# Seven half-wide products for two output blocks in six iterations of the last up projection

## The chip, the cores and the metric

The kernel runs on one core of a Trainium2 chip. The metric is the device time of one execution in microseconds (us), the median over runs; lower is better.

## What is computed

Three transformer blocks on 512 tokens of width 1024, all in float32, chained: a short convolution mixer, an attention block, and a block with gated linear attention beside window attention, each followed by a feed-forward part. The change lies in the last feed-forward part:

```python
h2 = _rms_norm(x, norm_ffn_g[l])
gu = h2 @ w_ffn_in[l]
ff_gate, ff_up = gu[..., :D_FF_2], gu[..., D_FF_2:]
x = x + (jax.nn.silu(ff_gate) * ff_up) @ w_ffn_out[l]
```

with h2 512 x 1024 and w_ffn_in 1024 x 5632 (D_FF_2 = 2816, which is 22 blocks of 128 columns on each side). The left half of the columns goes through silu (the "a" side, or silu side), the right half is the factor (the "g" side).

## The kernel before

Activations lie transposed: features on the 128 partitions, the 512 tokens along the free axis. Every float32 operand of a product is split into a high part (rounded to TensorE's fp32r form) and a low part (the rest), and each product is three matmuls: high weight by high activation, high weight by low activation, low weight by high activation. A *unit* of weights is one block of 128 output features by up to 1024 inputs (8 k tiles of 128 x 128, 512 KB). It takes this path:

- SyncE (SP) loads it into a landing buffer RAW (two of them in these phases, used in turn), as soon as GpSimd has split the unit that lay there.
- GpSimd (POOL) splits it into one slot of a ring of four (WH high, WL low): per half of the unit a TENSOR_SCALAR (L555, high) and a TENSOR_TENSOR (L558, low), four operations in all. It first waits until TensorE is through with the unit that lies in the slot. `WeightPhase` (L69) holds these counts; `owner` remembers the last unit of a slot over the borders of phases.
- TensorE (`unit`, L567 to L578) waits for the split, runs 8 x 3 matmuls of 128x512 into one PSUM bank and counts the unit as done.

The last up projection is phase `up2`: 11 iterations of four units (a, g, a, g), with banks 0 to 3, for two of the 22 blocks m. Its `body` (L639 on TensorE) waits before each unit until VectorE has emptied the bank. VectorE (DVE, `ffn`, L1794) multiplies the a result by the tokens' norm factor W[0] (L1804), then g (L1810), multiplies g by the silu of a (L1813) and makes the low part HL of that (L1815); ScalarE (ACT, L1321) makes the silu (L1328) and the high part HH (L1331). HH and HL, 44 KB a partition each, are filled block by block and feed the down projection. Every engine runs its own program in order; semaphores alone tie them together.

```python
pe.matmul(o, WH[s][:, k, :], xh[:, k0 + k, :], start=first and k == 0, stop=False)
pe.matmul(o, WH[s][:, k, :], xl[:, k0 + k, :], start=False, stop=False)
mm = pe.matmul(o, WL[s][:, k, :], xh[:, k0 + k, :], start=False, stop=last and k == nk - 1)
```

## Time and profile before

| | |
|---|---|
| median of 3 runs | 2083.39 us (2083.32 to 2083.63) |
| span of the profiled execution | 2081.4 us, so 2.0 us of the time lie outside the span |
| TensorE busy | 2074.3 us, 100% of the span |
| GpSimd busy | 1515.7 us, 73% |
| VectorE busy | 969.0 us, 47% |
| ScalarE busy | 499.3 us, 24% |

The span runs from the first to the last instruction of the profiled execution, whose own time stands nowhere else; the median of the runs stands for it. Busy is the union of an engine's instructions. A matmul's record is longer than the time until the next one may start, since matmuls are pipelined: what a matmul costs is read from the distance of two starts.

### The profile page before, as it was taken

The numbers are of one execution on the slowest core, as the hardware profiler recorded it, in microseconds if no ns is written. First come the engines' busy times: TensorE is split into PE (matmuls) and PEld (weight loads), VectorE is DVE, ScalarE is ACT, GpSimd is POOL, SyncE is SP. The second block draws the span as 40 slices with busy tenths as digits, with TensorE's granted clock in tenths as the row PEclk, the third lists the DMA queues.
The fourth block names the chain that finished last, engine by engine and source line by source line (L and its number), as shares of the span: only waits on it lengthen the run. The fifth ranks groups of instructions, "written<-read, shape, count | busy, mean of one in ns | idle before, by whom it ended". The sixth has DMA issues, their size and how long they took to land.

```text
span 2081.4 us, 28663 instructions
## 1 busy us (share of the span) xinstructions
PE 2074.3 (100%) x10112; PEld 1731.8 (83%) x10112; DVE 969.0 (47%) x1459; ACT 499.3 (24%) x999; POOL 1515.7 (73%) x1607
## 2 busy tenths in 40 slices
PE   9999999999999999999999999999999999999999
PEld 8888888888788878888888888889888888888887
DVE  6566655521456675655542166436753243222100
ACT  2002111100267673211100054222353122111000
POOL 7888888867865547888877775546545788777675
PEclk9999999999999999999999999999999999999999
DMA  5333333323333223333323332223222333333233
GB/s 158 101 89 102 95 101 91 101 84 93 106 108 86 82 82 86 91 101 91 100 86 94 100 90 81 62 71 102 72 68 69 87 110 93 99 93 101 86 91 96
DMA packets 368163, 192.45 MB, mean 92 GB/s; under 512 B 8672, under 2 KB 364608, under 8 KB 368080
## 3 DMA queue, kind: packets, MB, share of 16 engines
q1 hardware_dynamic: 365280, 186.52, 31.2%
q10 hardware_dynamic: 2800, 4.83, 0.7%
q8 instruction: 52, 0.85, 0.2%
q14 instruction: 31, 0.25, 0.0%
HBM read 189.19 MB, written 2.13 MB: 92 GB/s over the span
## 4 chain that ended last, share of the span: by engine, by line
PE 97%; DVE 2%; ACT 1%; DMA 0%; issue 0%; SPq 0%; DVEq 0%; ACTq 0%
PE PS L575 22%; PE PS L577 22%; PE PS L576 22%; PE PS L892 3%; PE PS L894 3%; PE PS L893 3%; PE PS L908 2%; PE PS L909 2%; PE PS L910 2%; PE PS L734 1%; PE PS L735 1%; PE PS L736 1%; PE PS L697 1%; PE PS L1091 1%; PE PS L677 1%; PE PS L762 1%
## 5 line engine op out<-in xcount | busy, mean ns | idle before, releaser
L558 POOL TENSOR_TENSOR RING<-RAW,RING 128x512 fp32r<-128x512 f32 x704 | 976.1, 1386 | 58.7
L555 POOL TENSOR_SCALAR RING<-RAW 128x512 fp32r<-128x512 f32 x704 | 519.6, 738 | 342.9 <-PE PS L894 89.9
L575 PE MATMUL PS<-XH,RING 128*128 128x512 f32 x1296 | 504.8, 389 | 0.0
L576 PE MATMUL PS<-XL,RING 128*128 128x512 f32 x1296 | 504.2, 389 | 0.0
L577 PE MATMUL PS<-XH,RING 128*128 128x512 f32 x1296 | 504.2, 389 | 0.0
L575 PEld LDWEIGHTS PS<-XH,RING 128*128 128x128 f32 x1296 | 243.3, 188 | 51.3 <-issue 1.1
L576 PEld LDWEIGHTS PS<-XL,RING 128*128 128x128 f32 x1296 | 243.3, 188 | 50.6 <-issue 0.2
L577 PEld LDWEIGHTS PS<-XH,RING 128*128 128x128 f32 x1296 | 243.3, 188 | 50.5
L575 PE MATMUL PS<-HH,RING 128*128 128x512 f32 x528 | 205.6, 389 | 0.0
L577 PE MATMUL PS<-HH,RING 128*128 128x512 f32 x528 | 205.4, 389 | 0.0
L576 PE MATMUL PS<-HL,RING 128*128 128x512 f32 x528 | 205.4, 389 | 0.0
L1785 DVE TENSOR_TENSOR XT<-PS,XT 128x512 f32<-128x512 f32 (+1 forms) x47 | 32.5, 692 | 325.7 <-PE PS L577 325.7
L553 POOL TENSOR_TENSOR COL<-COL 128x1 f32<-128x1 f32 x195 | 41.3, 212 | 147.1 <-PE PS L577 136.7
L1328 ACT ACTIVATE W<-W 128x512 f32<-128x512 f32 x66 | 41.7, 632 | 393.6 <-DVE W L1792 309.4
L577 PEld LDWEIGHTS PS<-HH,RING 128*128 128x128 f32 x528 | 99.1, 188 | 20.6
L575 PEld LDWEIGHTS PS<-HH,RING 128*128 128x128 f32 x528 | 99.1, 188 | 20.5
L576 PEld LDWEIGHTS PS<-HL,RING 128*128 128x128 f32 x528 | 99.1, 188 | 20.5
L1810 DVE TENSOR_TENSOR W<-PS,W 128x512 f32<-128x512 f32 x66 | 45.5, 690 | 147.0 <-PE PS L577 147.0
L1804 DVE TENSOR_TENSOR W<-PS,W 128x512 f32<-128x512 f32 x66 | 45.6, 691 | 129.8 <-PE PS L577 129.7
L1314 ACT ACTIVATE W<-XT 128x512 f32<-128x512 f32 (+1 forms) x40 | 25.3, 634 | 317.7 <-DVE XT L1785 242.1
L892 PE MATMUL PS<-XH,RING 128*128 128x512 f32 x232 | 95.2, 410 | 0.0
L908 PE MATMUL PS<-RING,XH 128*128 128x256 f32 x320 | 92.2, 288 | 0.0
(342 smaller groups left out, 3405.3 us busy)
## 6 DMA issues: line engine op xcount, KB each, us to landing
RAW<-in_ffn_w_up SPq DMA_DIRECT2D x88, 512.0 KB, 3.7
RAW<-in_w_in SPq DMA_DIRECT2D x52, 512.0 KB, 3.7
RAW<-in_w_ffn_in SPq DMA_DIRECT2D x44, 512.0 KB, 3.7
RAW<-in_ffn_w_down SPq DMA_DIRECT2D x32, 512.0 KB, 3.8
RAW<-in_a_w_in SPq DMA_DIRECT2D x24, 512.0 KB, 3.6
RAW<-in_b_w_qg SPq DMA_DIRECT2D x16, 512.0 KB, 3.6
RAW<-in_w_kvf SPq DMA_DIRECT2D x16, 512.0 KB, 3.9
RAW<-in_w_ffn_out SPq DMA_DIRECT2D x16, 512.0 KB, 3.7
```

The costliest lines, as they stand in the source:

```text
L555: hi = pool.tensor_scalar(WH[s][:, k0_:k1, :], RAW[r][:, k0_:k1, :], 1.0, 1.0, ALU.mult, ALU.mult)
L558: lo = pool.tensor_tensor(WL[s][:, k0_:k1, :], RAW[r][:, k0_:k1, :], WH[s][:, k0_:k1, :].bitcast(F32), ALU.subtract)
L575: pe.matmul(o, WH[s][:, k, :], xh[:, k0 + k, :], start=first and k == 0, stop=False)
L576: pe.matmul(o, WH[s][:, k, :], xl[:, k0 + k, :], start=False, stop=False)
L577: mm = pe.matmul(o, WL[s][:, k, :], xh[:, k0 + k, :], start=False, stop=last and k == nk - 1)
L892: pe.matmul(o, WH[s][:, k, :], xh[:, k, :], start=k == 0, stop=False)
L893: pe.matmul(o, WH[s][:, k, :], xl[:, k, :], start=False, stop=False)
L894: mm = pe.matmul(o, WL[s][:, k, :], xh[:, k, :], start=False, stop=k == KT - 1)
L908: pe.matmul(o, XH[:, k, c], RING[:, s:s + 2, 0, k, :], start=k == 0, stop=False)
L1328: act.activation(u, u, ACT.Silu).then_inc(sem("ffn_silu"), 1)
L1804: dve.tensor_tensor(a[:, 2:S + 2] if with_conv else u, PS[:, 2 * q, :], W[0][:, 0:S], ALU.mult).then_inc(sem("ffn_a"), 1)
L1810: dve.tensor_tensor(g, PS[:, 2 * q + 1, :], W[0][:, 0:S], ALU.mult).then_inc(sem("ffn_g"), 1)
```

## The change

Iterations 2 to 7 of `up2` (6 of 11) get a phase of their own, `seven2`, between two iterations of the old form and three of the old form (`rest2`).

In `seven2` the two a blocks (256 output features by 1024 inputs by 512 tokens) are made as a 2 x 2 by 2 x 2 product by Winograd's form of Strassen's scheme: seven products of quarters (128 outputs by 512 inputs by 256 tokens) in place of eight. Each is 4 k tiles x 3 matmuls of 128x256. The two g blocks keep their 128x512 matmuls, counted in halves of four k tiles. So an iteration has eleven *uses* of half a ring slot (`SEVEN_USES`), 7 + 4, and the ring is run as eight halves; uses 0 to 6 are the products. A use is freed by TensorE alone.

- Weights: both a units and both g units land in four RAW buffers. VectorE makes three sums of quarters (`add_weights`), GpSimd the fourth (right behind the low part of use 4, in place over a quarter of RAW0). ScalarE writes the high parts of all uses (`round_use`), GpSimd their low parts (`seven_low`).
- Activations: four combinations of quarters of the normed input, once for all six iterations, in HH's and HL's space that is still free: ScalarE one scaled quarter (four operations of 128x256) and the four high parts (128x1024), VectorE 16 operations of 128x256 and four low parts of 128x1024, between `body(0)` and `body(1)`.
- Results: ScalarE copies bank 0 after use 0 (`P1`) and after use 4; VectorE adds the products up (five operations of 128x256), multiplies the two sums by W[0] from SBUF, and goes on as before. Uses 4 and 6 add onto banks 0 and 3. TensorE waits before use 4 for the copy P1 (`taken`), before use 6 for VectorE's third sum.

Also the other semaphores are shared anew under fewer names; RAW has a fourth buffer; all six iterations are written out in every engine's program. The core of the diff:

```diff
+SEVEN = range(2, 8)
+SEVEN_USES = 11
+HALF = 256
...
+        TH = at("TH", [P, 4, 4, HALF], F32R, BIG + 28 * KB)
+        TL = at("TL", [P, 4, 4, HALF], F32R, BIG + 72 * KB)
+        TF = [at(f"TF{c}", [P, 4, HALF], F32, BIG + (8 + 4 * c) * KB) for c in range(5)]
+        SUM1, SUM2 = [at(f"SUM{k}", [P, 4, P], F32, W_at[8 + k]) for k in range(2)]
+        P1, U2, U3 = W[7][:, 0:HALF], W[7][:, HALF:S], W[1][:, 0:HALF]
...
+        def seven_phases(l):
+
+            ua, ug = [(up[l], 0, KT, col(q * P, 2 * P)) for q in range(2)], [(up[l], 0, KT, col(FF + q * P, 2 * P)) for q in range(2)]
+            plain = [ua[0], ug[0], ua[1], ug[1]]
+            a = wphase(4, SEVEN.start, plain)
+            b = wphase(4, len(SEVEN), ua + ug, landing=4, start=SEVEN.start)
+            stream["skip"] += b.U * b.iters
+            last = SEVEN_USES * len(SEVEN)
+            for slot in range(4):
+                of = []
+                for n in range(last - 8, last):
+                    if n % 8 // 2 == slot:
+                        t, q = divmod(n, SEVEN_USES)
+                        of.append(b.unit(SEVEN.start + t, 1 if q < 7 else 2 + (q - 7) // 2))
+                stream["owner"][slot] = max(of)
+            c = wphase(4, FT // 2 - SEVEN.stop, plain, start=SEVEN.stop)
+            return a, b, c
...
+        def ring_half(n):
+
+            h = n % 8
+            return h // 2, slice(h % 2 * 4, h % 2 * 4 + 4)
+
...
+        SEVEN_SRC = [RAW[0][:, 0:4, :], SUM2[:, :, :], RAW[1][:, 0:4, :], SUM1[:, :, :], RAW[0][:, 4:8, :], RAW[1][:, 4:8, :],
+                     RAW[0][:, 4:8, :], RAW[2][:, 0:4, :], RAW[2][:, 4:8, :], RAW[3][:, 0:4, :], RAW[3][:, 4:8, :]]
...
+            def seven_low(p):
+
+                for t in range(len(SEVEN)):
+                    for q in range(SEVEN_USES):
+                        n = SEVEN_USES * t + q
+                        s, k = ring_half(n)
+                        pool.wait_ge(sem("high_made"), KT + n + 1)
+                        lo = pool.tensor_tensor(WL[s][:, k, :], SEVEN_SRC[q], WH[s][:, k, :].bitcast(F32), ALU.subtract)
+                        lo.then_inc(use_count(p, n, sem("low_made"), split_done, 9, KT)[0], 2 if q == 6 else 1)
+                        if q == 4:
+                            pool.wait_ge(sem("low_made"), use_count(p, n, sem("low_made"), split_done, 9, KT)[1])
+                            pool.tensor_tensor(RAW[0][:, 4:8, :], SUM2[:, :, :], RAW[0][:, 4:8, :], ALU.subtract).then_inc(
+                                sem("low_made"), 1)
...
+            def seven_products(l):
+
+                p = ph["seven2"]
+                xs = [(XH[:, 0:4, 0:HALF], XL[:, 0:4, 0:HALF]), (TH[:, 1], TL[:, 1]), (TH[:, 2], TL[:, 2]), (TH[:, 0], TL[:, 0]),
+                      (XH[:, 4:8, 0:HALF], XL[:, 4:8, 0:HALF]), (TH[:, 3], TL[:, 3]), (XH[:, 4:8, HALF:S], XL[:, 4:8, HALF:S])]
+                bank = (0, 1, 2, 3, 0, 4, 3)
+                for t, i in enumerate(SEVEN):
+                    m = l * FT + 2 * i
+                    for q in range(7):
+                        n = SEVEN_USES * t + q
+                        s, ks = ring_half(n)
+                        pe.wait_ge(*use_count(p, n, sem("low_made"), split_done, 9, KT))
+                        if q == 4:
+                            pe.wait_ge(sem("taken"), TB + 2 * t + 1)
+                        elif q == 6:
+                            pe.wait_ge(sem("combined"), KT + 5 * t + 3)
+                        elif t == 0:
+                            if q < 4:
+                                pe.wait_ge(sem(("ffn_a", "ffn_g")[q % 2]), m - 1 + q // 2)
+                            if q == 1:
+                                pe.wait_ge(sem("xld"), scaled(4) + KT + 4)
+                        elif q == 0:
+                            pe.wait_ge(sem("taken"), TB + 2 * t)
+                        else:
+                            pe.wait_ge(sem("combined"), KT + 5 * t - 5 + {1: 1, 2: 2, 3: 5, 5: 4}[q])
+                        xh, xl = xs[q]
+                        o = PS[:, bank[q], 0:HALF]
+                        for k in range(4):
+                            w = ks.start + k
+                            on = q in (4, 6)
+                            pe.matmul(o, WH[s][:, w, :], xh[:, k, :], start=not on and k == 0, stop=False, skip_group_check=on)
+                            pe.matmul(o, WH[s][:, w, :], xl[:, k, :], start=False, stop=False, skip_group_check=on)
+                            mm = pe.matmul(o, WL[s][:, w, :], xh[:, k, :], start=False, stop=k == 3, skip_group_check=on)
+                        mm.then_inc(use_count(p, n, sem("used"), unit_done, 8, 2 * KT)[0], 2 if q == 6 else 1)
+                    for u in range(2):
+                        if t > 0:
+                            pe.wait_ge(sem("ffn_g"), m - 1 + u)
+                        for h in range(2):
+                            n = SEVEN_USES * t + 7 + 2 * u + h
+                            s, ks = ring_half(n)
+                            pe.wait_ge(*use_count(p, n, sem("low_made"), split_done, 9, KT))
+                            o = PS[:, 5 + u, :]
+                            for k in range(4):
+                                w, x = ks.start + k, 4 * h + k
+                                pe.matmul(o, WH[s][:, w, :], XH[:, x, :], start=h == 0 and k == 0, stop=False)
+                                pe.matmul(o, WH[s][:, w, :], XL[:, x, :], start=False, stop=False)
+                                mm = pe.matmul(o, WL[s][:, w, :], XH[:, x, :], start=False, stop=h == 1 and k == 3)
+                            mm.then_inc(use_count(p, n, sem("used"), unit_done, 8, 2 * KT)[0], 1)
...
+                    for i in range(SEVEN.start):
+                        body(i)
+                    seven_products(l)
+                    pu = ph["rest2"]
+                    loop(pe, FT // 2, body, start=SEVEN.stop)
...
+                def round_use(n):
+
+                    p = ph["seven2"]
+                    t, q = divmod(n, SEVEN_USES)
+                    i = p.start + t
+                    s, k = ring_half(n)
+                    if n >= 8:
+                        act.wait_ge(*use_count(p, n - 8, sem("used"), unit_done, 8, 2 * KT))
+                    else:
+                        act.wait_ge(unit_done, p.owner[s] + 1)
+                    if q == 0:
+                        act.wait_ge(loaded[0], 16 * p.load_count(i, 0))
+                    elif q < 4:
+                        act.wait_ge(sem("seven_added"), 3 * t + 4 + (2, 3, 1)[q - 1])
+                    elif q == 6:
+                        act.wait_ge(sem("low_made"), KT + 9 * t + 6)
+                    elif q in (7, 9):
+                        act.wait_ge(loaded[2 + (q - 7) // 2], 16 * p.load_count(i, 2 + (q - 7) // 2))
+                    act.copy(WH[s][:, k, :], SEVEN_SRC[q]).then_inc(sem("high_made"), 1)
...
+                def seven():
+
+                    for t, i in enumerate(SEVEN):
+                        more = t + 1 < len(SEVEN)
+                        n, nx = SEVEN_USES * t, SEVEN_USES * (t + 1)
+                        round_use(n + 7)
+                        act.wait_ge(sem("used"), 2 * KT + 8 * t + 1)
+                        if t > 0:
+                            act.wait_ge(sem("combined"), KT + 5 * t - 4)
+                        act.copy(P1, PS[:, 0, 0:HALF]).then_inc(sem("taken"), 1)
...
+                    operands_high()
+                    silu(1, 0)
+                    round_use(0)
+                    high(1, 0)
+                    round_use(1)
+                    round_use(2)
+                    round_use(3)
+                    silu(1, 1)
+                    round_use(4)
+                    round_use(5)
+                    high(1, 1)
+                    round_use(6)
+                    seven()
...
+                def add_weights(t):
+
+                    p = ph["seven2"]
+                    i = p.start + t
+                    for s in range(2):
+                        dve.wait_ge(loaded[s], 16 * p.load_count(i, s))
+                    if t > 0:
+                        dve.wait_ge(sem("low_made"), KT + 9 * (t - 1) + 6)
+                    a11, a21, a22 = RAW[0][:, 0:4, :], RAW[1][:, 0:4, :], RAW[1][:, 4:8, :]
+                    dve.tensor_tensor(SUM1[:, :, :], a21, a22, ALU.add).then_inc(sem("seven_added"), 1)
+                    dve.wait_ge(sem("seven_added"), 3 * t + 5)
+                    dve.tensor_tensor(SUM2[:, :, :], SUM1[:, :, :], a11, ALU.subtract).then_inc(sem("seven_added"), 1)
+                    dve.tensor_tensor(a21, a11, a21, ALU.subtract).then_inc(sem("seven_added"), 1)
...
+                        dve.wait_ge(sem("taken"), TB + 2 * t + 1)
+                        dve.wait_ge(sem("used"), 2 * KT + 8 * t + 2)
+                        dve.tensor_tensor(U2, PS[:, 1, 0:HALF], P1, ALU.add).then_inc(done, 1)
+                        if t > 0:
+                            low(i - 1, 1)
+                        dve.wait_ge(done, KT + 5 * t + 1)
+                        dve.wait_ge(sem("used"), 2 * KT + 8 * t + 3)
+                        dve.tensor_tensor(U3, PS[:, 2, 0:HALF], U2, ALU.add).then_inc(done, 1)
+                        dve.wait_ge(done, KT + 5 * t + 2)
+                        dve.wait_ge(sem("used"), 2 * KT + 8 * t + 4)
+                        dve.tensor_tensor(u[1][:, HALF:S], U3, PS[:, 3, 0:HALF], ALU.subtract).then_inc(done, 1)
+                        dve.wait_ge(sem("used"), 2 * KT + 8 * t + 6)
+                        dve.tensor_tensor(u[1][:, 0:HALF], PS[:, 4, 0:HALF], U3, ALU.add).then_inc(done, 1)
+                        if t + 1 < len(SEVEN):
+                            add_weights(t + 1)
+                        dve.wait_ge(unit_done, ph["seven2"].unit(i, 1) + 1)
+                        dve.wait_ge(sem("ffn_h"), l * FT + 2 * i)
+                        dve.tensor_tensor(u[0][:, HALF:S], U2, PS[:, 3, 0:HALF], ALU.subtract).then_inc(done, 1)
+                        dve.wait_ge(done, KT + 5 * t + 5)
+                        dve.wait_ge(sem("taken"), TB + 2 * t + 2)
+                        for q in range(2):
+                            dve.tensor_tensor(u[q], u[q], W[0][:, 0:S], ALU.mult).then_inc(sem("ffn_a"), 1)
+                        gated(i, 0)
+                        low(i, 0)
...
+                    body(0)
+                    operands(0)
+                    operands(1)
+                    operand_low(0)
+                    operands(2)
+                    operand_low(1)
+                    operands(3)
+                    operand_low(2)
+                    operand_low(3)
+                    body(1)
+                    seven()
+                    pu = ph["rest2"]
+                    loop(dve, FT // 2, body, steps, start=SEVEN.stop)
```

GpSimd's program where `rest2` begins. Before, the same place is inside the phase's loop, and each unit is like this one:

```order
L550 ISA [waits unit_done]
L553 TENSOR_TENSOR COL_55<-COL_55 128x1 [waits weights_loaded0]
L555 TENSOR_SCALAR RING_64<-RAW0_60 128x512
L557 ISA
L558 TENSOR_TENSOR RING_64<-RAW0_60,RING_64 128x512 [waits weights_high]
L555 TENSOR_SCALAR RING_64<-RAW0_60 128x512
L557 REGISTER_ALU
L558 TENSOR_TENSOR RING_64<-RAW0_60,RING_64 128x512 [waits weights_high]
```

Now (L598 and L602 are `seven_low`, L621 and L624 the split):

```order
L602 TENSOR_TENSOR RAW0_60<-SUM1_96,RAW0_60 128x512 [waits low_made]
L598 TENSOR_TENSOR RING_64<-RAW1_61,RING_64 128x512 [waits high_made]
L598 TENSOR_TENSOR RING_64<-RAW0_60,RING_64 128x512 [waits high_made]
L598 TENSOR_TENSOR RING_64<-RAW2_62,RING_64 128x512 [waits high_made] x2
L598 TENSOR_TENSOR RING_64<-RAW3_63,RING_64 128x512 [waits high_made] x2
L621 TENSOR_SCALAR RING_64<-RAW0_60 128x512 [waits weights_loaded0,unit_done]
L624 TENSOR_TENSOR RING_64<-RAW0_60,RING_64 128x512 [waits weights_high]
L621 TENSOR_SCALAR RING_64<-RAW0_60 128x512
L624 TENSOR_TENSOR RING_64<-RAW0_60,RING_64 128x512 [waits weights_high]
```

The last L598 make the low parts of uses 62 to 65; the first L621 writes ring slot 0, which uses 64 and 65 fill, so its `unit_done` is the last g unit of `seven2`.

ScalarE's program from the start of `seven2`'s weights (L1478 is `round_use`, uses 0 to 8 in order; L1453 a silu, L1458 a high part of H, L1502 the copy P1; the buffer printed as SUM1 is the code's SUM2, SUM0 its SUM1):

```order
L1478 CAST RING_64<-RAW0_60 128x512 [waits weights_loaded0,unit_done]
L1458 CAST HH_86<-W5_68 128x512 [waits ffn_h]
L1478 CAST RING_64<-SUM1_96 128x512 [waits seven_added,unit_done]
L1478 CAST RING_64<-RAW1_61 128x512 [waits seven_added,unit_done]
L1478 CAST RING_64<-SUM0_95 128x512 [waits seven_added,unit_done]
L1453 ACTIVATE W4_67<-W4_67 128x512 [waits ffn_a]
L1478 CAST RING_64<-RAW0_60 128x512 [waits unit_done]
L1478 CAST RING_64<-RAW1_61 128x512 [waits unit_done]
L1458 CAST HH_86<-W6_69 128x512 [waits ffn_h]
L1478 CAST RING_64<-RAW0_60 128x512 [waits low_made,unit_done]
L1478 CAST RING_64<-RAW2_62 128x512 [waits weights_loaded2,unit_done]
L1502 COPY W7_70<-PS 128x256 [waits used]
```

Before, ScalarE had only the silu and the high part there for each block; the copy P1 now stands behind use 6, which waits for GpSimd's fourth sum (`low_made`).

## Rows read from the trace of the kernel before

**Rows 1.** The page: span, busy times, engines of the chain that ended last.
```profile
span 2081.4 us, 28663 instructions
PE 2074.3 (100%) x10112; PEld 1731.8 (83%) x10112; DVE 969.0 (47%) x1459; ACT 499.3 (24%) x999; POOL 1515.7 (73%) x1607
PE 97%; DVE 2%; ACT 1%; DMA 0%; issue 0%; SPq 0%; DVEq 0%; ACTq 0%
```

**Rows 2.** Up projection's stretch: length, busy us PE PEld DVE ACT POOL, clock, DMA.
```profile
1722.00:1960.00 238.00, 238.00 (x1052) 197.10 (x1051) 67.87 (x93) 32.05 (x49) 183.97 (x210) 1.00 0.33 96
```

**Rows 3.** Timeline of TensorE, unit of 24 matmuls: start, duration, engine, line.
```profile
1726.04 0.39 PE L575 MATMUL PS<-XH,RING 128*128 128x512 f32 x1
...
1731.48 0.39 PE L575 MATMUL PS<-XH,RING 128*128 128x512 f32 x1
```

**Rows 4.** Timeline of TensorE, 45 matmuls of 128x256 in a row.
```profile
1219.30 0.28 PE L908 MATMUL PS<-RING,XH 128*128 128x256 f32 x1
...
1224.58 0.28 PE L910 MATMUL PS<-RING,XL 128*128 128x256 f32 x1
```

**Rows 5.** Groups of GpSimd, VectorE and ScalarE by form: busy us, mean ns.
```profile
L558 POOL TENSOR_TENSOR RING<-RAW,RING 128x512 fp32r<-128x512 f32 x680 | 953.2, 1402 | 56.7
L555 POOL TENSOR_SCALAR RING<-RAW 128x512 fp32r<-128x512 f32 x680 | 503.9, 741 | 342.9 <-PE PS L894 89.9 <-PE PS L577 76.1 <-PE PS L910 62.8
L1331 ACT CAST HH<-W 128x512 f32 x60 | 37.3, 622 | 200.9 <-DVE W L1813 200.9
L1534 ACT ACTIVATE SQ<-PS 128x256 f32<-128x256 f32 x16 | 5.9, 382 | 15.9 <-PE PS L987 15.9
L1815 DVE TENSOR_TENSOR HL<-W,HH 128x512 f32 x60 | 48.5, 808 | 54.5 <-ACT HH L1331 54.5
L1804 DVE TENSOR_TENSOR W<-PS,W 128x512 f32<-128x512 f32 x66 | 45.6, 691 | 129.8 <-PE PS L577 129.7
L1813 DVE TENSOR_TENSOR W<-W,W 128x512 f32<-128x512 f32 x66 | 50.3, 762 | 3.2 <-ACT W L1328 1.2
L2402 DVE SCALAR_TENSOR_TENSOR XL<-PS,PRM,XH 128x256 fp32r<-128x256 f32 x16 | 6.8, 478 | 3.8 <-ACT XH L1688 3.8
L1856 DVE CUSTOM_DVE_ANT_0 PROB<-PS,W 128x512 f32<-128x512 f32 x16 | 10.4, 689 | 21.0 <-PE PS L677 21.0
L1856 DVE CUSTOM_DVE_ANT_0 PROB<-PS,W 128x256 f32<-128x256 f32 x16 | 6.6, 417 | 0.0
```

**Rows 6.** One line's durations, ns min/median/max: VectorE with both tensors in SBUF.
```profile
L1771 DVE SCALAR_TENSOR_TENSOR XL<-XT,PRM,XH x40: 826/1094/1777, 153.5 to 1717.4; 128x512 fp32r<-128x512 f32 x28, - x12
```

**Rows 7.** VectorE and TensorE at the end of iteration 0 and of iteration 1.
```profile
1739.26 1.01 DVE L1815 TENSOR_TENSOR HL<-W,HH 128x512 fp32r<-128x512 f32 x1 [0.69 <-ACT HH L1331]
1758.68 0.39 PE L575 MATMUL PS<-XH,RING 128*128 128x512 f32 x1
```

**Rows 8.** From a unit's last matmul to the split that it frees, and the split.
```profile
1742.13 0.39 PE L577 MATMUL PS<-XH,RING 128*128 128x512 f32 x1
...
1742.71 0.19 POOL L553 TENSOR_TENSOR COL<-COL 128x1 f32<-128x1 f32 x1 [0.57 <-PE PS L577]
1742.86 0.62 POOL L555 TENSOR_SCALAR RING<-RAW 128x512 fp32r<-128x512 f32 x1
...
1745.52 1.29 POOL L558 TENSOR_TENSOR RING<-RAW,RING 128x512 fp32r<-128x512 f32 x1
```

**Rows 9.** The end: TensorE's last 128x512 matmul, then stretches with their clock.
```profile
2077.11 0.39 PE L577 MATMUL PS<-HH,RING 128*128 128x512 f32 x1
2077.88 0.92 PE L619 MATMUL PS<-IDF,XT 128*128 128x128 f32 x4 [0.38 <-DVE XT L1825]
...
2079.50:2080.00 0.50, 0.00 (x0) 0.00 (x0) 0.00 (x0) 0.00 (x0) 0.00 (x0) 1.00 0.72 221
2080.00:2080.50 0.50, 0.00 (x0) 0.00 (x0) 0.00 (x0) 0.00 (x0) 0.00 (x0) 0.84 0.80 238
2080.50:2081.00 0.50, 0.00 (x0) 0.00 (x0) 0.00 (x0) 0.00 (x0) 0.00 (x0) 0.50 0.23 66
```

More of the change, by code:

```diff
@@ L69, with __init__ @@
 class WeightPhase:
-    def __init__(self, stream, ring, iters, units, first=0, landing=2):
-        self.first = first
+    def __init__(self, stream, ring, iters, units, first=0, landing=2, start=0):
+        self.first, self.start = first, start
         self.ring, self.iters, self.units, self.U = ring, iters, units, len(units)
@@ L520, in body @@
                                 load_parameters()
-                loop(sp, p.iters, body)
+                if p is ph["seven2"]:
+                    for i in SEVEN:
+                        body(i)
+                else:
+                    loop(sp, p.start + p.iters, body, start=p.start)
             for part in range(2):
@@ L1332, in ffn, with silu, high @@
-                loop(act, FT // 2, body, steps)
+                        silu(i, q)
+                        act.wait_ge(sem("prm_ready"), 4)
+                        high(i, q)
+                def silu(i, q):
+                    m = 2 * i + q
+                    u = W[3 + q][:, 0:S]
+                    act.wait_ge(sem("ffn_u" if conv else "ffn_a"), m + (l * FT + 1))
+                    act.activation(u, u, ACT.Silu).then_inc(sem("ffn_silu"), 1)
+                def high(i, q):
+                    m = 2 * i + q
+                    act.wait_ge(sem("ffn_h"), m + l * FT + 1)
+                    act.copy(tile(HH, m), W[5 + q][:, 0:S]).then_inc(sem("ffn_high"), 1)
@@ new lines, in seven_operands, with operands_high @@
+                def seven_operands():
+                    act.wait_ge(sem("resid"), tiles(n) + KT)
+                    for k in range(4):
+                        cp = act.activation(TF[0][:, k, :], XT[:, k, HALF:S], ACT.Copy, scale=PRM[:, R_FFN2 + k:R_FFN2 + k + 1])
+                    cp.then_inc(sem("xhd"), 1)
+                def operands_high():
+                    for c in range(4):
+                        act.wait_ge(sem("seven_added"), c + 1)
+                        act.copy(TH[:, c], TF[1 + c][:, :, :]).then_inc(sem("xhd"), 1)
@@ new lines, in ffn @@
+                if l == 2:
+                    silu(0, 0)
+                    seven_operands()
+                    act.wait_ge(sem("prm_ready"), 4)
+                    high(0, 0)
+                    silu(0, 1)
+                    high(0, 1)
+                    operands_high()
[11 more added lines that the diff above has]
+                    seven()
+                    loop(act, FT // 2, body, steps, start=SEVEN.stop)
+                else:
+                    loop(act, FT // 2, body, steps)
```

146 lines of the change are left out of this document (111 added, 35 removed).

## Prediction

> **What bounds the kernel now.** I read the page's head first: TensorE is busy 2074.3 of 2081.4 us, and 97% of the chain that ended last is TensorE's own [rows 1]. Then the stretch of the change: from 1722 to 1960 us TensorE is busy all 238.00 us at granted clock 1.00, GpSimd 183.97, VectorE 67.87, ScalarE 32.05 [rows 2]. So nothing there waits for weights or for a bank; the end moves one for one with what TensorE is given to do, and with any hole that is torn into its row. Third, the timeline for the price of a matmul, since the 389 ns of its record overlap the next. Between the starts of two 128x512 matmuls 24 apart lie 1731.48 - 1726.04 = 5.44 us [rows 3], 0.2267 us each. For 128x256 44 steps take 5.28 us [rows 4], 0.1200 us each: half the columns cost 53%, not 50%.
>
> **The change part by part.**
>
> *Products.* Two a blocks took 2 x 24 x 0.2267 = 10.88 us. Seven products are 7 x 12 = 84 matmuls of 128x256: 84 x 0.1200 = 10.08 us. The g blocks keep their matmuls. Gain 0.80 us an iteration, **-4.8 us** in six. Those of rows 4 have the activations as the loaded side; both sides are 128 wide and loaded anew each time, so I take the same distance. The Trainium skill ("TensorE: Matmul & The Clock Gate", section "Wait — 56ns, not 53.3ns?") puts the distance of warm matmuls at columns / 2.4 GHz plus about 2.5 ns. By that, as an estimate, the products would fall from 10.36 to 9.17 us and six iterations would gain 7.1 us, which would make the forecast below 2.3 us lower. Both rows 3 and rows 4 lie above that rule (0.2267 against 0.2158, 0.1200 against 0.1092), so the rows decide.
>
> *Steady iterations.* TensorE now has 10.08 + 10.88 = 20.96 us in each. GpSimd: 12 TENSOR_TENSOR x 1.402 = 16.8 us [rows 5]. ScalarE: 11 high parts, 2 silus, 2 parts of HH, each 0.62, and 2 copies x 0.38 = 10.1. VectorE: five sums of 128x256 at 0.42, two evictions at 0.69, and nine operations of 128x512 from SBUF at 0.76 to 0.81 [rows 5]: some 10.5. All fit. The copy P1 is needed 3 x 1.44 = 4.3 us after use 0 ends and takes 0.4; VectorE's third sum is needed 2 x 1.44 = 2.9 us after use 3 ends and takes 0.4. Loads for the next iteration start at GpSimd's use 6, some 20 us ahead. Cost nothing; if VectorE's or ScalarE's row of work got 2 us late, use 6 would be the one to wait.
>
> *Entry.* This is not steady: all weights of the first iteration must be made while VectorE has the activation sums in front of it. It is free after `low(0, 1)` at 1739.26 + 1.01 = 1740.27 [rows 7]. Then come:
> - 16 operations of 128x256, scaled and with both tensors in SBUF. No row has that shape. From below 0.42 (6.8 us / 16, from PSUM, back to back [rows 5]); from above the median of the 128x512 form, 1.09 [rows 6], less 0.27 for 256 columns (0.689 - 0.417 [rows 5]) = 0.82. The smallest 128x512 one, 0.83, gives 0.56. GpSimd, which stretches these, is idle here, since the ring is full. I take 0.50: 8.0 us.
> - four of 128x1024: 0.69 + 2 x 0.27 = 1.23 each, 4.9 us. Now 1753.2.
> - block 2's share of `body(1)`: two evictions 1.38, the product 0.76, waiting 0.9 for HH (54.5 / 60), the low part 0.81 [rows 5]: 3.85. Now 1757.0.
> - `add_weights(0)`: SUM1 and SUM2, 2 x 0.76. Now 1758.6.
>
> From SUM2 on: ScalarE's high part of use 1, 0.62; GpSimd's low parts of uses 1, 2, 3, 4 and the fourth sum, 5 x 1.40 = 7.0; ScalarE's high parts of uses 6 and 7 and then P1, 1.62. With 0.2 for the hand-overs P1 is there at 1768.0. TensorE begins `seven2` where iteration 2 begins now, 1758.68 [rows 7], and without a wait would begin use 4 at + 4 x 1.44 = 1764.4. So it loses **+3.6 us** ahead of use 4; shorter holes before use 1 are part of the same sum. Ends: 1.7 us if VectorE's 16 go at 0.42 and GpSimd's at 1.29 [rows 8]; 9 if the 16 take 0.82. The order of ScalarE's rows makes this: P1 needs nothing of use 6, but stands behind it.
>
> *Exit.* `rest2`'s first unit goes into slot 0. Uses 64 and 65, the last two, fill both its halves (64 mod 8 = 0), so GpSimd must wait until TensorE is through with the whole last g unit, and TensorE then waits for the whole split. Slots 1 to 3 have been free for long, but GpSimd works in order. From the last matmul's start: 0.39 to its end, 0.19 until GpSimd moves [rows 8], the split 2 x (0.741 + 1.402) = 4.29 [rows 5], 0.1 to TensorE; less the 0.23 that the next matmul would have waited anyway: **+4.7 us**. Ends: 4.4 with a split as short as in rows 8 (1742.86 to 1746.81, 3.95 us), 5.5 if VectorE stretches each of the four by 0.2. Behind it GpSimd needs 4.3 us a unit against TensorE's 5.44, so no second hole.
>
> *Clock.* No stretch before has a hole of this size. What the trace has is its end: the last dense matmul starts at 2077.11, eight transposes follow, and between 2080.0 and 2080.5 the granted clock goes from 1.00 towards 0.50 [rows 9], 2.4 GHz to 1.2 GHz, about 2.8 us after the dense row ends. The exit's hole is longer. I take that the clock falls in it and is at half for some 2.8 us of matmuls after it, of which half is lost: **+1.4 us**, an estimate from those rows. From below nothing; from above 4, if it falls at both holes and stays low for longer.
>
> *Nothing elsewhere:* the renamed semaphores are waited for at the same places; the written-out code is fetched beside a full queue, and other parts of TensorE's program are written out in the same way.
>
> Sum: -4.8 + 3.6 + 4.7 + 1.4 = **+4.9 us** on the span of 2081.4. The profiled execution's own time is not shown; with the 2.0 us outside the span it would be the median, so 2083.4 + 4.9 = **2088.3 us**.
>
> **The rivals.** A measurement of this kernel can tell about 0.2%, 4.2 us, from no change: the bounds are 2079.2 and 2087.6.
>
> (a) *The clock holds.* The first two holes are as sized, nothing is half speed: +3.5 us, 2086.9, no difference. For it: in mid-run the trace has no hole above 2 us at TensorE, so nothing shows that one of 4.7 is enough. Against: the fall at the end [rows 9]. The Trainium skill ("TensorE: Matmul & The Clock Gate", section "HAM oscillation — how this bites in real kernels") says that idle gaps of this order throttle TensorE; that rule gives the forecast, not this rival.
>
> (b) *Not slower: the entry chain is short.* It rests on VectorE's 16 operations. At 0.42 each, with GpSimd's at 1.29, P1 is there at 1766.1 and the entry costs 1.7 us: -4.8 + 1.7 + 4.4, with the clock kept, is +1.3, 2084.7. Even with the clock falling the sum is under 4.2 us if the entry costs under 2.9, so it decides from about 0.45 us an operation on down. For it: GpSimd is idle there. Against: the scale and the second tensor in SBUF, whose cheapest 128x512 row is 0.83, not 0.69.
>
> (c) *A new steady bound.* GpSimd and VectorE stretch each other: 1.29 against 1.402 us for the same operation [rows 5, 8], and 0.83 to 1.78 [rows 6]. VectorE gets five more operations on SBUF tensors per iteration. If each iteration loses 1 us before use 4 or 6, and the entry goes by 0.7 an operation (+3.2): 4.9 + 3.2 + 5 = +13, 2096. Against: 4 us of slack at GpSimd, 10 at the others.
>
> (d) *Faster by over 4.2 us* would need the exit's hole away, and it follows from the slot count alone. The change does do what it says: the seven products are in TensorE's program.
>
> **How the numbers follow.** Forecast 0.48, (a) 0.22, (b) 0.14, (c) 0.13, something faster that I don't see 0.03. Within the forecast some lies under 2087.6, as some of (a) lies above it. Slower by over 0.2%: 0.59; within: 0.37; faster: 0.04. The range runs from just under (b), 2084.0, to 2094.5, the forecast with the entry and the exit near their upper ends (+5.4 and +0.8), which leaves out most of (c).
>
> **What would show it.** In the new profile: (1) starts of 128x256 matmuls 0.120 us apart, seven products 10.1 us; (2) at TensorE one hole, or two in a row, of 3.6 us together within the first eight us of `seven2`, the last released by ScalarE's copy at L1502; (3) none in the following five iterations; (4) one hole of 4.7 us at the first unit of `rest2`, released by GpSimd's L624; (5) a granted clock of 0.50 for some us behind (4). The prediction is wrong if (4) is missing, if (3) shows a wait in each iteration, or if the sum of holes is under 4 us.

## The result, and the profile after

| | median us | range | runs |
|---|---|---|---|
| before | 2083.49 | 2083.20 to 2083.63 | 6 |
| the change | 2089.72 | 2088.39 to 2092.36 | 6 |

The medians differ by 6.2 us. The ratio, here and below that of the means, is 1.0032, with a 95% interval of 1.0022 to 1.0042: slower, clear of the noise. The profiled execution took 2090.37 us, its span is 2088.6, 7.2 more than before. The runs lie 4.0 us apart where those of before lie 0.4 apart. Two later runs of the kernel before, of 4246 and 6397 us, are left out of the ratios.

The head of the profile's page and the stretch of the up projection, the lines that answer to [rows 1, 2]:

```profile
span 2088.6 us, 28877 instructions
PE 2074.1 (99%) x10328; PEld 1741.3 (83%) x10328; DVE 1026.3 (49%) x1527; ACT 546.0 (26%) x1085; POOL 1512.6 (72%) x1551
PE 95%; DVE 2%; ACT 1%; POOL 1%; issue 0%; DMA 0%; SPq 0%; DVEq 0%; ACTq 0%; POOLq 0%
...
1722.00:1960.00 238.00, 229.96 (x1235) 200.19 (x1235) 123.60 (x158) 78.21 (x134) 182.66 (x155) 0.99 0.32 94
```

TensorE was busy all 238 us of that stretch and now is for 229.96: 8 us of holes, and the granted clock is no longer 1.00. The list of TensorE's waits names both holes; none of its other waits is above 1.1 us (engine and line that waited, releaser, us, times, longest):

```profile
PE PS L641 <- POOL RING L624: 5.1, 1, 5.1
PE PS L733 <- ACT W L1502: 2.9, 1, 2.9
```

Now the two places in TensorE's timeline (start, duration, line). The entry, ahead of use 4 of the first iteration:

```profile
1764.50 0.28 PE L735 MATMUL PS<-TH,RING 128*128 128x256 f32 x1
1767.72 0.36 PE L733 MATMUL PS<-XH,RING 128*128 128x256 f32 x1 [2.94 <-ACT W L1502]
...
1769.01 0.41 PE L735 MATMUL PS<-XH,RING 128*128 128x256 f32 x1
1769.23 0.41 PE L733 MATMUL PS<-XH,RING 128*128 128x256 f32 x1
```

The copy P1 (L1502) comes last in a chain: GpSimd's fourth sum (L602) releases ScalarE's high parts of uses 6 and 7 (L1478), and the copy stands behind them:

```profile
1764.82 1.26 POOL L602 TENSOR_TENSOR RAW<-SUM,RAW 128x512 f32<-128x512 f32 x1
1766.17 1.14 ACT L1478 CAST RING<-RAW 128x512 fp32r<-128x512 f32 x2 [3.63 <-POOL RAW L602]
1767.21 0.36 ACT L1502 COPY W<-PS 128x256 f32<-128x256 f32 x1
```

And the exit, at the first unit behind the phase, with GpSimd's split of that unit, which starts only when the last g unit is done:

```profile
1889.16 0.39 PE L749 MATMUL PS<-XH,RING 128*128 128x512 f32 x1
1894.65 0.73 PE L641 MATMUL PS<-XH,RING 128*128 128x512 f32 x1 [5.10 <-POOL RING L624]
1895.18 0.63 PE L642 MATMUL PS<-XL,RING 128*128 128x512 f32 x1
...
1889.64 0.62 POOL L621 TENSOR_SCALAR RING<-RAW 128x512 fp32r<-128x512 f32 x1 [13.81 <-PE PS L749]
1890.34 1.79 POOL L624 TENSOR_TENSOR RING<-RAW,RING 128x512 fp32r<-128x512 f32 x1
1892.11 1.05 POOL L621 TENSOR_SCALAR RING<-RAW 128x512 fp32r<-128x512 f32 x1
1893.24 1.26 POOL L624 TENSOR_TENSOR RING<-RAW,RING 128x512 fp32r<-128x512 f32 x1
```

The distance of starts is 3.22 us at the first, where 0.12 would do, and 5.49 at the second, where 0.23 would do. Behind each the matmuls are slow: 0.21 us apart for 128x256 (0.12 before), 0.43 for 128x512. The granted clock of these stretches (length, busy of TensorE, weight loads, VectorE, ScalarE, GpSimd, then the clock, DMA share, GB/s):

```profile
1768.00:1770.00 2.00, 2.00 (x13) 2.00 (x12) 0.88 (x3) 1.13 (x3) 2.00 (x3) 0.60 0.10 30
1770.00:1772.00 2.00, 2.00 (x12) 2.00 (x11) 0.00 (x0) 0.37 (x1) 2.00 (x2) 0.55 1.08 323
1772.00:1774.00 2.00, 2.00 (x17) 1.96 (x16) 0.73 (x2) 0.62 (x1) 2.00 (x3) 1.00 1.15 348
...
1896.00:1898.00 2.00, 2.00 (x6) 1.58 (x5) 0.00 (x0) 0.00 (x0) 1.92 (x3) 0.50 0.81 239
1898.00:1900.00 2.00, 2.00 (x10) 1.58 (x9) 0.00 (x0) 0.00 (x0) 1.92 (x3) 0.98 0.16 47
```

So the clock falls at both holes, to half of 2.4 GHz. It does not fall at once: at the entry it is still 1.00 from 1767 to 1768 us, when TensorE is working again, and 0.70 from 1768 to 1769. The account of the profiled execution against [rows 1], from the distances of starts: holes and short hitches at the entry 3.4, slow matmuls behind them 16 x 0.095 = 1.5; exit 5.3; slow matmuls behind it 1.7 (eight distances, seven of them 0.2 too long and one 0.3); the products -4.8: together +7.1, measured +7.2.

Nothing else in the phase costs. From the start of the second iteration at 1784.49 to the end of the last g block, 1889.39, five iterations take 104.9 us, 20.98 each, against 20.96 worked out.

### The profile page after: what moved, and what is told of

Read it like the earlier page. It is cut to its first block, busy times and chain, and to the rows that moved or that the text cites. A ratio compares the mean times of both kernels' runs of the same rounds, so it can differ in the third digit from the quotient of the medians.

```text
span 2088.6 us, 28877 instructions
## 1 busy us (share of the span) xinstructions
PE 2074.1 (99%) x10328; PEld 1741.3 (83%) x10328; DVE 1026.3 (49%) x1527; ACT 546.0 (26%) x1085; POOL 1512.6 (72%) x1551
## 4 chain that ended last, share of the span: by engine, by line
PE 95%; DVE 2%; ACT 1%; POOL 1%; issue 0%; DMA 0%; SPq 0%; DVEq 0%; ACTq 0%; POOLq 0%
PE PS L641 20%; PE PS L642 20%; PE PS L643 20%; PE PS L1012 3%; PE PS L1014 3%; PE PS L1013 3%; PE PS L1028 2%; PE PS L1029 2%; PE PS L1030 2%; PE PS L854 1%; PE PS L856 1%; PE PS L855 1%; PE PS L748 1%; PE PS L747 1%; PE PS L749 1%; PE PS L733 1%
## 5 line engine op out<-in xcount | busy, mean ns | idle before, releaser
L624 POOL TENSOR_TENSOR RING<-RAW,RING 128x512 fp32r<-128x512 f32 (+1 forms) x656 | 909.1, 1386 | 54.7
L621 POOL TENSOR_SCALAR RING<-RAW 128x512 fp32r<-128x512 f32 (+1 forms) x656 | 482.0, 735 | 361.1 <-PE PS L1014 90.1
L641 PE MATMUL PS<-XH,RING 128*128 128x512 f32 x1104 | 430.9, 390 | 5.1 <-POOL RING L624 5.1
L642 PE MATMUL PS<-XL,RING 128*128 128x512 f32 x1104 | 430.2, 390 | 0.0
L643 PE MATMUL PS<-XH,RING 128*128 128x512 f32 x1104 | 430.0, 389 | 0.0
L641 PEld LDWEIGHTS PS<-XH,RING 128*128 128x128 f32 x1104 | 207.6, 188 | 49.9 <-issue 6.6
L643 PEld LDWEIGHTS PS<-XH,RING 128*128 128x128 f32 x1104 | 207.6, 188 | 43.3
L642 PEld LDWEIGHTS PS<-XL,RING 128*128 128x128 f32 x1104 | 207.6, 188 | 43.0 <-issue 0.2
L1453 ACT ACTIVATE W<-W 128x512 f32<-128x512 f32 x66 | 41.7, 633 | 358.3 <-DVE W L2009 309.3
L619 POOL TENSOR_TENSOR COL<-COL 128x1 f32<-128x1 f32 x163 | 35.8, 219 | 113.6 <-PE PS L643 107.3
L1012 PE MATMUL PS<-XH,RING 128*128 128x512 f32 x232 | 95.2, 410 | 0.0
L1014 PE MATMUL PS<-XH,RING 128*128 128x512 f32 x232 | 90.7, 391 | 0.0
L1030 PE MATMUL PS<-RING,XL 128*128 128x256 f32 x320 | 90.5, 283 | 0.0
```

What stands on the lines that cost most here:

```text
L621: hi = pool.tensor_scalar(WH[s][:, k0_:k1, :], RAW[r][:, k0_:k1, :], 1.0, 1.0, ALU.mult, ALU.mult)
L624: lo = pool.tensor_tensor(WL[s][:, k0_:k1, :], RAW[r][:, k0_:k1, :], WH[s][:, k0_:k1, :].bitcast(F32), ALU.subtract)
L1012: pe.matmul(o, WH[s][:, k, :], xh[:, k, :], start=k == 0, stop=False)
L1014: mm = pe.matmul(o, WL[s][:, k, :], xh[:, k, :], start=False, stop=k == KT - 1)
L1030: mm = pe.matmul(o, XL[:, k, c], RING[:, s:s + 2, 0, k, :], start=False, stop=k == KT - 1)
L1453: act.activation(u, u, ACT.Silu).then_inc(sem("ffn_silu"), 1)
```

## The experiments

Ten kernels ran. The kernels of before that ran with them had medians of 2083.46, 2083.50 and 2083.54. All medians below stand against these.

### The exit: whose slot, and in what order

The theory says that the hole is a matter of slots: the first unit wants slot 0 just after slot 0 was used last.

**e1_exit.** The last three iterations use the slots in the order 1, 2, 3, 0.

```diff
-            c = wphase(4, FT // 2 - SEVEN.stop, plain, start=SEVEN.stop)
+            c = wphase(4, FT // 2 - SEVEN.stop, plain, first=1, start=SEVEN.stop)
```

> The three last iterations of the up projection take the ring slots in the order 1, 2, 3, 0 instead of 0, 1, 2, 3; nothing else. Theory (slot 0 is still in use by the last g block, and GpSimd works in order): the hole of 5.3 us at the first unit behind the seven-product phase is gone, and with it the half-speed matmuls behind it (1.9 us in the profiled run): about 2082.5 us, 7.2 under the change. Rival (the hole is made by the switch itself, by loads or by how the splits are issued after the phase): the hole stays at 4 us or more and the time stays within 1 us of the change's 2089.7.

Measured: 2091.21 us (2090.19 to 2092.19), ratio 1.0036 (1.0021 to 1.0050). By the time alone the rival looks better than the theory, which said 2082.5: nothing is gained, and the time is even 1.5 us above that of the change. The trace says otherwise. TensorE is busy and at clock 1.00 through the place of the old hole, and the hole stands 67 us later, at the first unit of the down projection (length, TensorE busy, clock, DMA, GB/s; then TensorE's and GpSimd's timeline):

```profile
1888.00:1892.00 4.00, 4.00 (x19) 1.00 0.37 109
...
1956.17 0.39 PE L643 MATMUL PS<-XH,RING 128*128 128x512 f32 x1
1961.60 0.77 PE L641 MATMUL PS<-HH,RING 128*128 128x512 f32 x1 [5.05 <-issue]
...
1956.65 0.62 POOL L621 TENSOR_SCALAR RING<-RAW 128x512 fp32r<-128x512 f32 x1 [16.81 <-PE PS L643]
```

GpSimd had idled for 16.8 us until the last up unit was done. The view names no releaser for TensorE ("issue"), but GpSimd's split of that unit ends at 1961.50 us, just ahead of its first matmul. My edit had made its own repeat: with the order 1, 2, 3, 0 the last unit of the up projection lies in slot 0, and the down projection begins with slot 0. The same mechanism, one border further on. Of the 1.5 us over the change about 1.1 are slow matmuls behind the entry's hole, which is as long as before (3.22 us): in this trace the half clock lasts longer there.

**f1_slots.** e1_exit, and the down projection's three slots are shifted too (`first=1` in the call that makes `down2`: 1, 2, 0).

> As e1_exit, and the last down projection too takes its ring slots shifted by one (1, 2, 0 instead of 0, 1, 2). In e1_exit the hole of 5.0 us left the switch behind the seven products and stood at the first unit of the down projection, which wants slot 0 right behind a unit in slot 0. Theory (a hole wherever the first unit of a phase lands in the slot that was used last): with both shifted there is no such hole at either place; only the entry's 2.9 us and its slow matmuls are left: 2089.7 less 5.3 and less about 2, so about 2082.5. Rival (the hole comes from leaving a full ring and would move on once more): 2089 or more, with a hole of 5 us elsewhere.

Measured: 2083.68 us (2081.84 to 2084.72), ratio 1.0000 (0.9991 to 1.0009). One wait of TensorE is left in the whole up projection, the entry's 2.94 us. That is 6.0 us less than the change for two arguments that move no work, 1.2 above what was expected and far from the rival. The expectation had taken the exit's slow matmuls of one profiled execution off a median. By the distances of starts the entry costs 4.8 us here, 3.4 of waits and 1.4 of slow matmuls, and 2083.5 - 4.8 + 4.8 is 2083.5.

**f4_five.** The opposite way to the same test: the slots stay, the count of uses changes. `SEVEN = range(2, 7)`, so 55 uses.

> Seven products in iterations 2 to 6 only, five of them; nothing else changed. 55 uses end in slot 3, and slot 0 was last filled by uses 48 and 49, the fifth and sixth of the last iteration. Theory: no hole behind the phase, the gain is 5 x 0.8 = 4.0, the entry costs what it did (3.4 and about 1.5): 2083.5 - 4.0 + 4.9 = about 2084.4. Rival (the hole behind the phase does not depend on the slot): 2090 or more.

Measured: 2084.90 us (2083.19 to 2086.47), ratio 1.0007 (0.9998 to 1.0016). No hole at the exit, the entry's 2.93 us as before; expected was about 2084.4. So what made it was that 66 uses leave a remainder of 2 over eight halves, and GpSimd waits in order.

### The entry: one chain through three engines

**e2_p1.** In the first iteration alone ScalarE's copy P1 stands behind use 5 rather than behind use 7.

```diff
                     round_use(5)
+                    act.wait_ge(sem("used"), 2 * KT + 1)
+                    act.copy(P1, PS[:, 0, 0:HALF]).then_inc(sem("taken"), 1)
                     high(1, 1)
...
-                        act.wait_ge(sem("used"), 2 * KT + 8 * t + 1)
...
+                        if t > 0:
+                            act.wait_ge(sem("used"), 2 * KT + 8 * t + 1)
```

> In the first of the six iterations alone ScalarE makes the copy P1 right behind the high part of use 5, ahead of those of uses 6 and 7. Theory (P1 only waits because it stands behind use 6, which waits for GpSimd's fourth sum): the 2.9 us wait before use 4 goes; GpSimd's own row then ends last, with some 0.3 us before use 4 and 0.9 us before use 5, and the clock does not fall there: 3.4 + 1.5 less 1.3, so about 2086 us, 3.6 under the change. Rival (GpSimd's row of low parts is the real bound, the copy only ends last by a little): at most 1 us gained, 2088.7 or more.

Measured: 2088.10 us (2087.45 to 2089.05), ratio 1.0022 (1.0013 to 1.0032), 1.6 less than the change. In its trace the starts before use 4 are 0.30 us apart and before use 5 1.18, nearly the two waits expected, and the clock stays at 1.00 there. So the entry gained 3.2 us in this trace, but the time fell by 1.6 and met neither the theory's 2086 nor the rival's 2088.7. In the second iteration TensorE waited 0.7 us for the copy P1. There VectorE's weight sums began behind a load, at 1776.22 us, where in g1_copy, which has the same entry, they began at 1774.90. And the exit, 5.49 us as before, was followed by eleven slow distances where the change has eight:

```profile
1894.00:1896.00 2.00, 2.00 (x6) 0.50 0.80 233
1896.00:1898.00 2.00, 2.00 (x7) 0.62 0.12 34
```

The clock had also fallen sooner: 0.67 from 1890 to 1892 us, 3.1 us behind the end of TensorE's last matmul, where in the change's trace it was 1.00 until 1894. What one hole costs behind itself thus depends on more than its length, and a difference of two versions that both keep the exit's hole is uncertain by it. From here on I judged entry edits on top of f1_slots.

**e3_both.** e1_exit and e2_p1 together.

> Both edits, the ring slots 1, 2, 3, 0 behind the phase and the early copy P1. Theory (the two holes are independent and each costs its length and its slow matmuls): 2089.7 - 7.2 - 3.6 = about 2079 us, faster than the kernel before by some 4. Rival (TensorE regains in one place what it lost in the other, or the clock loss does not add): no more than the larger gain of the two alone, 2082.5.

Measured: 2087.67 us (2086.91 to 2088.60), ratio 1.0020 (1.0010 to 1.0030). The entry's part came (3.5 us under e1_exit, where theory had 3.6). The expected 2079 was missed because the exit's hole stood at the down projection, as in e1_exit, for the same reason.

**g1_copy.** f1_slots with the early copy.

> f1_slots plus the early copy P1 of e2_p1 alone; VectorE's sums and the rest of ScalarE's order as in the change. Theory (with P1 out of the way GpSimd's row of low parts is what TensorE waits for, 0.2 us before use 4 and 1.1 before use 5 as in e2_p1; holes of 1 us do not lower the clock): 2079.0 + 1.6 = about 2080.5, spread under 1 us. Rival (GpSimd's row costs as much as the copy did): 2082 or more.

Measured: 2080.51 us (2080.13 to 2080.78), ratio 0.9985 (0.9976 to 0.9994). That is the expected number, and 3.2 us under f1_slots for the place of one copy of 0.36 us. By the two traces 1.7 of it are the wait and 1.4 the slow matmuls behind it.

**e4_sums.** VectorE makes the weight sums at the head of iteration 1's share (the condition reads `and q == 0` in place of `and q == 1`).

> VectorE makes the three weight sums of the first iteration at the start of its share of iteration 1, ahead of block 2, instead of behind it; ScalarE's order is unchanged. Theory (the entry is one chain from VectorE's sums to P1): SUM2 is there some 3.8 us earlier, so P1 is there at about 1763.8, before TensorE needs it at 1764.4; no hole, no fall of the clock: 3.4 + 1.5 = 4.9 us less, about 2084.8. Rival (ScalarE's row holds the chain, since uses 1 to 7 stand between its silus and high parts, which still wait for VectorE's block 3): less than 1.5 us gained.

Measured: 2090.28 us (2089.37 to 2091.54), ratio 1.0032 (1.0019 to 1.0044): nothing gained. The sums were early (SUM2 from 1753.64 us, 3.7 sooner), but the row behind them was not, and P1 starts at 1767.01 where it did at 1767.21:

```profile
1754.86 0.68 DVE L2111 TENSOR_TENSOR W<-PS,W 128x512 f32<-128x512 f32 x1
1755.57 0.63 ACT L1453 ACTIVATE W<-W 128x512 f32<-128x512 f32 x1 [3.87 <-DVE W L2111]
1756.11 0.61 ACT L1478 CAST RING<-RAW 128x512 fp32r<-128x512 f32 x1
1756.79 1.36 POOL L598 TENSOR_TENSOR RING<-RAW,RING 128x512 fp32r<-128x512 f32 x1 [14.65 <-ACT RING L1478]
...
1764.61 1.26 POOL L602 TENSOR_TENSOR RAW<-SUM,RAW 128x512 f32<-128x512 f32 x1
1765.96 1.14 ACT L1478 CAST RING<-RAW 128x512 fp32r<-128x512 f32 x2 [3.63 <-POOL RAW L602]
1767.01 0.36 ACT L1502 COPY W<-PS 128x256 f32<-128x256 f32 x1
```

The first high part (L1478) stands behind block 2's silu (L1453), which waits for the eviction (L2111) that the sums now delay. GpSimd begins at 1756.79, and its five low parts and fourth sum end at 1765.87. So the rival's number held, and its cause in kind: ScalarE's order. But the link was block 2's silu ahead of use 0, not block 3. In the change this second way had time to spare: GpSimd made use 0's low part from 1754.77 us and then idled for 2.66 us until use 1's high part, made from SUM2, was there. The early sums pushed use 0 back by 2.0 us, and in this trace GpSimd has no idle time between use 0 and the fourth sum, while from 1742.1 to 1756.8 it had nothing to do.

**f3_order.** f1_slots, the early sums, and ScalarE in this order: high parts of uses 0 to 4, block 2's silu and high part, use 5, block 3's silu, P1, the rest.

```diff
                     operands_high()
-                    silu(1, 0)
                     round_use(0)
-                    high(1, 0)
                     round_use(1)
                     round_use(2)
                     round_use(3)
-                    silu(1, 1)
                     round_use(4)
+                    silu(1, 0)
+                    high(1, 0)
                     round_use(5)
+                    silu(1, 1)
+                    act.wait_ge(sem("used"), 2 * KT + 1)
+                    act.copy(P1, PS[:, 0, 0:HALF]).then_inc(sem("taken"), 1)
                     high(1, 1)
```

> f1_slots, with VectorE's three weight sums of the first iteration ahead of block 2 (as e4_sums) and ScalarE's order there changed: high parts of uses 0 to 4 first, then block 2's silu and high part, use 5, block 3's silu, the copy P1, and then the rest. In e4_sums the sums were 3.7 us earlier but GpSimd began only 2 us before TensorE needed it, since use 0 stood behind block 2's silu, and its seven operations in a row ended at 1765.8. Theory (the entry is GpSimd's row of low parts, started by ScalarE's first high part): it starts 4 us earlier, no hole at either end, clock 1.00 throughout: 2083.5 - 4.8 = about 2078.7, faster than the kernel before. Rival (the sums and ScalarE's row delay the evictions that TensorE waits for, a new hole of over 1 us): 2080 or more.

Measured: 2078.97 us (2078.56 to 2079.22), ratio 0.9978 (0.9968 to 0.9987). TensorE is back at 100%, and the chain's shares are those of [rows 1]:

```profile
span 2077.3 us, 28877 instructions
PE 2069.9 (100%) x10328; PEld 1738.0 (84%) x10328; DVE 1028.6 (50%) x1527; ACT 545.4 (26%) x1085; POOL 1516.9 (73%) x1551
```

This is the fastest version: 4.5 us, or 0.2%, under the kernel before, and 10.8 under the change. The time came as expected; the way there did so only in part. GpSimd began its row 4.3 us earlier than in e4_sums (1752.51), but its fourth sum ended only 2.1 us earlier (1763.77). Its low part of use 0 and VectorE's first sum now ran side by side, and took 1.86 and 1.78 us, where in e4_sums they took 1.36 and 0.68:

```profile
1752.51 1.86 POOL L598 TENSOR_TENSOR RING<-RAW,RING 128x512 fp32r<-128x512 f32 x1 [10.15 <-ACT RING L1478]
...
1753.14 1.78 DVE L2043 TENSOR_TENSOR SUM<-RAW 128x512 f32<-128x512 f32 x1
```

The largest distance of two starts of TensorE in the up projection is 0.34 us.

**g2_start.** f3_order with the copy P1 back behind uses 6 and 7: which half of the new order did it?

> f3_order with the copy P1 put back behind the high parts of uses 6 and 7; the early sums and the early high parts of uses 0 to 4 stay. Theory (P1 comes 1.2 us of ScalarE and 0.1 behind GpSimd's fourth sum, which in f3_order ended at 1763.8): P1 is there at about 1765.3, TensorE wants it at 1764.4, one hole of 0.9 us and no slow matmul: about 2079.9. Rival (P1's place in the row is what made the 2.9 us whatever the start): 2082 or more.

Measured: 2080.68 us (2079.85 to 2080.94), ratio 0.9985 (0.9976 to 0.9994). P1 begins at 1766.17 and the wait is 1.33 us, not 0.9. GpSimd's fourth sum was done at 1764.02, but ScalarE first waited for VectorE's block 3:

```profile
1764.60 0.62 ACT L1458 CAST HH<-W 128x512 fp32r<-128x512 f32 x1 [1.84 <-DVE W L2120]
1765.13 1.13 ACT L1478 CAST RING<-RAW 128x512 fp32r<-128x512 f32 x2
1766.17 0.36 ACT L1502 COPY W<-PS 128x256 f32<-128x256 f32 x1
```

The early copy alone leaves waits of about 0.2 and 1.1 us (g1_copy), the early sums and high parts alone one of 1.33, and in neither trace is a matmul slow. Both together leave next to nothing. Early high parts without early sums did not run, so what the high parts give by themselves is not shown.

### The clock by itself

**f2_fill.** The change, with matmuls that nobody needs in both holes.

```diff
+                        if t == 0 and q == 4:
+                            for _ in range(10):
+                                pe.matmul(PS[:, 7, :], ONE[:, :].bitcast(F32R), XH[:, 0, :], start=True, stop=True)
...
                     seven_products(l)
+                    for _ in range(20):
+                        pe.matmul(PS[:, 7, :], ONE[:, :].bitcast(F32R), XH[:, 0, :], start=True, stop=True)
```

> The change with 10 extra 128x512 matmuls (2.3 us) on TensorE ahead of its wait before use 4 of the first iteration and 20 (4.5 us) ahead of the first unit behind the phase, into a bank that nobody reads; they fit into the two holes and give nothing to the result. Theory (the half-speed matmuls come from the idle time in the two holes, and the runs' spread of 4 us from how much of them each run gets): the holes keep their outer length, the clock stays 1.00, the time is 2083.5 - 4.8 + 3.4 + 5.3 = about 2087.4 and the spread falls under 1 us. Rival (the clock falls for another reason, or the holes alone make the time): 2089.7 as the change, same spread.

Measured: 2087.72 us (2087.52 to 2088.19), ratio 1.0020 (1.0011 to 1.0030). Expected was 2087.4. The holes are about as long as ever from useful matmul to useful matmul (3.12 and 5.55 us), the clock is 1.00 in every run:

```profile
1764.00:1768.00 4.00, 3.48 (x20) 2.69 (x18) 0.01 (x1) 1.45 (x4) 3.92 (x4) 1.00 0.01 2
1888.00:1894.00 6.00, 5.50 (x25) 4.18 (x24) 2.40 (x3) 0.62 (x1) 5.28 (x5) 1.00 0.01 1
```

30 useless matmuls make the kernel 2.0 us faster and the runs agree within 0.7 us. So of the change's 6.2 us some 2.0 are the clock (2.3 by the means; with six runs of the change, 4 us apart, this is no more exact than about 1 us), and nearly all of the 4 us between its runs is the clock too. Both holes were filled at once, so the share of each is known only from the profiled executions.

## Why the prediction was right

Forecast 2088.3, measured 2089.7; the case held likeliest, both holes and a fallen clock, is what happened. Step by step:

- **Products, -4.8.** Right. Starts are 0.120 us apart in the new products, and f3_order, which has next to no holes, lies 4.5 us under the kernel before. The distance of matmuls that the Trainium skill states ("TensorE: Matmul & The Clock Gate", section "Wait — 56ns, not 53.3ns?"), which the forecast set aside for the rows, would have made it 7.1, an estimate; the traces do not agree with it.
- **Steady iterations, 0.** Right on the whole: 20.98 us each. The one late P1 in e2_p1 (0.7 us, second iteration, behind a late load) says that the slack there is smaller than I had it. GpSimd's operations took 1.47 us in the phase, not 1.40: 1.27 at the least and 1.82 at the most, the long ones beside VectorE's operations on SBUF tensors.
- **Entry, +3.6.** Right: 3.4, with P1 at 1767.2 to 1767.6 where I had it at 1768.0. The 16 operations of 128x256 took 3.05 + 3 x 1.67 = 8.1 us against 8.0, and that was luck. The forecast took 0.50 each because GpSimd, which stretches them, would be idle. Fourteen started about 0.40 us apart, which is the 0.42 of rival (b); but GpSimd was still splitting until 1742.06, and beside it the first two took 0.83 and 1.51 us where the others took 0.47 to 0.49. Had these two been like the others, the sums would have come some 1.4 us earlier, an estimate from these rows, and the entry been cheaper by up to as much. What I had not seen is the second way to P1, over use 0, which stands behind a silu; it decides as soon as the sums come earlier (e4_sums). That P1's place in the row makes the wait was right (g1_copy).
- **Exit, +4.7.** Right in its cause, 0.6 short. The split took 4.86 us (1889.64 to 1894.50) and not the mean of 4.29: VectorE finishes block 15 in just that time, and two of the four operations, those beside its two operations on SBUF tensors, took 1.79 and 1.05 us; the other two took 0.62 and 1.26, as short as in [rows 8]. The upper end, 5.5, had named this.
- **Clock, +1.4.** The term that was too small. I let the clock fall at the exit alone; it falls at the entry's 2.9 us as well, in four of the five profiled executions that have this hole unfilled. It cost 1.5 and 1.7 us in the change's profiled execution, some 2.0 for both in the medians (f2_fill). For the exit 1.4 was near; the entry's share was missing.

Of the rivals, (a) fails: the clock did not hold. (b) fails in its sum, 8.1 us and not 6.7, but was right on the price of an undisturbed operation. (c) fails, no steady wait: all five later iterations together lost 0.1 us. (d) fails: the exit's hole came as the slot count says. With both holes gone the products do give over 4.2 us, 4.5 in f3_order. Of the signs, (1) to (5) are all there; the hole of (2) ends nine us into the phase, not within eight.

The errors 3.4 - 3.6, 5.3 - 4.7 and about 2.0 - 1.4 make up +1.0 of the 1.4 us by which the forecast was low.

My first mend of the exit was wrong where the prediction was right: I looked at the border that I changed and not at the next one, which has the same rule.

## What to carry to other kernels

A product scheme that saves one eighth of the matmuls of one side, here 0.8 of 21.8 us an iteration, is worth it only if the borders of its stage cost less than the sum of these gains, so price the first and the last iteration apart from the steady one: which operation in each in-order queue stands behind one that it doesn't need, and which buffer does the next phase want first. When a ring is left at an odd place, start the next phase at the slot that was freed longest ago, and check every later border for the same clash. When a mend brings nothing, look in the trace whether the hole is gone or has moved before giving up the theory.

## What the hardware showed that I had not expected

- **Small holes cost more than their length, and not the same each time.** With one hole of 2.93 us and no other (f4_five) the profiled run kept clock 1.00; with one of 2.94 us (f1_slots) it fell to 0.50. TensorE's work up to the hole was the same in both. The stretch behind the hole in f4_five, then in f1_slots:

```profile
1768.00:1770.00 2.00, 2.00 (x18) 1.00 0.05 16
```

```profile
1768.00:1770.00 2.00, 2.00 (x10) 0.50 0.05 15
```

  The runs of these two spread over 3.3 and 2.9 us, those without a hole above 1.6 us over 0.7 (f3_order, g1_copy) and 1.1 (g2_start). The change, with two holes, spreads over 4.0. A spread of 3 to 4 us where the kernel before stays within 1.5 in every batch is itself a sign of such holes; its lack is no proof of none, since e2_p1 and e3_both, with a hole of over 5 us each, spread over 1.6 and 1.7. The Trainium skill ("TensorE: Matmul & The Clock Gate", section "HAM oscillation — how this bites in real kernels") warns of idle gaps of a few us; the runs agree for 5 us, where the clock fell in each trace that has the hole unfilled, and show that at 2.9 us it falls in some executions and not in others. What decides it is not shown.
- **How far into a hole the clock falls differs too:** 1.9 us behind the end of TensorE's last matmul at the entry of e4_sums, 2.6 in f1_slots, and in the change only after TensorE had gone on; at the hole of over 5 us, 2.0 us behind it in e1_exit, 3.1 in e2_p1 and 5.1 in the change.
- **A gap of 1.0 to 1.5 us did not lower it** in any profiled run here (e2_p1, e3_both, g1_copy, g2_start).
- **Useless matmuls paid:** 30 of them, put where TensorE had nothing to do, took some 2.0 us off the kernel.
